# Second attention of a two-block transformer: blocks of 128 and of 256 keys share one step

## The reference, cut to what matters

```python
# NSA heads: a compressed branch, and two branches of softmax attention with a
# linear distance bias (here both see all of the 512 keys)
s = einsum('bgrqd,bgnd->bgrqn', q, k) * ATTN_SCALE - slopes * dist
p = softmax(where(dist >= 0, s, NEG_INF))
o = gate * einsum('bgrqn,bgnd->bgrqd', p, v)
...
# stick-breaking heads: the weight of key j is its sigmoid times the product of
# (1 - sigmoid) over the keys between j and the query
w[q, j] = sigmoid(s[q, j]) * prod(1 - sigmoid(s[q, l]) for l in (j, q))
o = einsum('qj,jd->qd', w, v)
```

## Time and profile before

| what | value |
|---|---|
| time, median of 3 runs | 1500.35 us (1496.9 to 1500.56) |
| the profiled execution: its time, its span | 1499.78 us, 1497.7 us |
| PE busy | 1453.9 us (97% of the span) |
| DVE busy | 948.2 us (63%) |
| ACT busy | 416.8 us (28%) |
| chain of work that ended last | PE 88%, DVE 7%, ACT 2%, issue 2% |
| second attention on PE (first scores to last output) | 760.30 to 984.60 us |

### The profile page before, as it was taken

How to read it: one execution, slowest core, us unless ns; L and a number is a source line. 1 busy time by engine, 2 the same in 40 slices (tenths; PEclk the granted TensorE clock), 3 DMA queues, 4 the chain that set the end, 5 groups by cost and what they waited for, 6 DMA issues and landing times.

```text
span 1497.7 us, 19514 instructions
## 1 busy us (share of the span) xinstructions
PE 1453.9 (97%) x7218; PEld 1171.0 (78%) x7218; DVE 948.2 (63%) x1705; ACT 416.8 (28%) x880; POOL 95.0 (6%) x75
## 2 busy tenths in 40 slices
PE   5999988999999999999999999999999999999997
PEld 5888866778888888888866666778887888888886
DVE  8787698876766665656556667874555445444443
ACT  5435444331111110003244456421113222221011
POOL 0000000110000000325200000000030000000110
PEclk9999999999999999999999999999999999999999
DMA  9353332445555655433211111123332223323332
GB/s 371 110 173 126 131 100 80 139 128 185 193 196 185 206 180 157 148 102 105 79 63 43 52 48 43 43 78 97 108 98 70 98 98 96 101 85 105 91 90 93
DMA packets 52609, 175.79 MB, mean 117 GB/s; under 512 B 5952, under 2 KB 6336, under 8 KB 52544
## 3 DMA queue, kind: packets, MB, share of 16 engines
q1 hardware_dynamic: 52544, 174.94, 35.7%
HBM read 172.82 MB, written 2.10 MB: 117 GB/s over the span
## 4 chain that ended last, share of the span: by engine, by line
PE 88%; DVE 7%; ACT 2%; issue 2%; DMA 0%; POOL 0%; SPq 0%; ACTq 0%; DVEq 0%
PE bank L650 20%; PE bank L652 19%; PE bank L651 19%; PE bank L1144 7%; PE bank L1163 2%; PE bank L1175 2%; PE bank L1198 2%; PE bank L826 2%; PE bank L824 2%; PE bank L825 2%; PE bank L997 1%; PE bank L858 1%; DVE wl L1694 1%; DVE ada L1714 1%; PE bank L662 1%
## 5 line engine op out<-in xcount | busy, mean ns | idle before, releaser
L650 PE MATMUL bank<-uh,wh 128*128 128x512 f32 x808 | 316.1, 391 | 6.0 <-DVE wl L1694 4.8
L651 PE MATMUL bank<-ul,wh 128*128 128x512 f32 x808 | 315.2, 390 | 0.0
L652 PE MATMUL bank<-uh,wl 128*128 128x512 f32 x808 | 315.2, 390 | 0.0
L1692 DVE CAST wh<-wraw 128x1024 fp32r<-128x1024 f32 (+1 forms) x223 | 147.9, 663 | 192.8 <-PE bank L652 179.9
L1694 DVE TENSOR_TENSOR wl<-wraw,wh 128x1024 fp32r<-128x1024 f32 (+1 forms) x223 | 260.3, 1167 | 7.7
L650 PEld LDWEIGHTS bank<-uh,wh 128*128 128x128 f32 x808 | 152.1, 188 | 39.0 <-issue 4.9
L652 PEld LDWEIGHTS bank<-uh,wl 128*128 128x128 f32 x808 | 152.1, 188 | 31.8
L651 PEld LDWEIGHTS bank<-ul,wh 128*128 128x128 f32 x808 | 152.0, 188 | 31.3
L650 PE MATMUL bank<-hh,wh 128*128 128x512 f32 x352 | 137.6, 391 | 0.0
L652 PE MATMUL bank<-hh,wl 128*128 128x512 f32 x352 | 137.1, 389 | 0.0
L651 PE MATMUL bank<-hl,wh 128*128 128x512 f32 x352 | 137.0, 389 | 0.0
(11 more groups left out here) (352 smaller groups left out, 2297.1 us busy)
## 6 DMA issues: line engine op xcount, KB each, us to landing
ada<-in_w_ada_dram SPq DMA_DIRECT2D x96, 512.0 KB, 4.6
wraw<-in_w_in_dram SPq DMA_DIRECT2D x61, 512.0 KB, 3.3
wraw<-in_w_ffn_gate_dram SPq DMA_DIRECT2D x44, 512.0 KB, 3.3
wraw<-in_w_ffn_up_dram SPq DMA_DIRECT2D x44, 512.0 KB, 3.3
wraw<-in_w_ffn_down_dram SPq DMA_DIRECT2D x32, 512.0 KB, 3.5
wraw<-in_w_ffn_down_dram SPq DMA_DIRECT2D x16, 384.0 KB, 3.1
wraw<-in_w_out_dram SPq DMA_DIRECT2D x16, 256.0 KB, 2.8
wraw<-in_w_out_dram SPq DMA_DIRECT2D x8, 512.0 KB, 3.4
```

What stands on the lines that cost most here:

```text
L650: nc.tensor.matmul(bank[:], a, rh[:, k0 + k, :], start=(first and k == 0), stop=False)
L651: nc.tensor.matmul(bank[:], a, rl[:, k0 + k, :], start=False, stop=False)
L652: mm = nc.tensor.matmul(bank[:], b, rh[:, k0 + k, :], start=False, stop=(last and k == nk - 1))
L1692: V.tensor_copy(wh[:, slot, 0:n], wraw[:, slot, 0:n]).then_inc(w_hi, 1)
```

## The change

The blocks of 128 and of 256 keys of one pair and branch now share a step: `PARTS = ((0, 1), (2,), (3,))`. Their scores stand side by side in one bank (columns 0 to 127 and 128 to 383, `place`), and so do their weights in `zt`, `kp`, `rb` and `wt2`. A pair and branch takes 3 steps of 384, 384 and 512 columns in place of 4 of 128, 256, 384 and 512; there are 24 NSA steps and 12 stick-breaking ones. The operations that need one row of bias, maximum, sum or running product for each query block (L2317, L1619, L2334, L2342, L2353, L2357) are still issued once for each block and head; the copies L1610 and the sigmoids L1630 and L1632 go over a step's columns in one instruction, and so do the small L2321, L2329 and L2331. Every step of attention now takes 12 fill matmuls, and two steps of 24 come behind the last one (`PORTIONS`). The number of matmuls, transposes and fill matmuls is the same as before.

```diff
-        NSA_TILES, ATT_TILES = 32, 48
+        NSA_TILES, ATT_TILES = 24, 36
+        PARTS = ((0, 1), (2,), (3,))
-        PORTIONS = [8, 8, 8, 12, 6, 6, 12, 12] * 4 + [8] * 3 + [12] * 12 + [8] * 3
+        PORTIONS = [12] * ATT_TILES + [24] * 2
...
+        def span_of(m):
+            return 512 if m % 3 == 2 else 384
+        def place(m, i):
+            first = P if i == 1 else 0
+            return slice(first, first + ZLEN[i])
...
             def pair_scores(m):
-                for ab in range(2):
...
-                    mm = nc.tensor.matmul(B[4 + 2 * (m % 2) + ab][:, 0:ZLEN[i]], q[:, i * P:(i + 1) * P], k[:, 0:ZLEN[i]],
-                                          start=True, stop=True)
+                for i in parts:
+                    for ab in range(2):
...
+                        mm = nc.tensor.matmul(B[4 + 2 * (m % 2) + ab][:, place(m, i)], q[:, i * P:(i + 1) * P],
+                                              k[:, 0:ZLEN[i]], start=True, stop=True)
                 mm.then_inc(a_z, 1)
...
             def pair_turn(m):
-                    for j in range(i + 1):
+                    for j in range(span_of(m) // P):
...
             def pair_output(m):
-                for j in range(i + 1):
+                for i, j in ((i, j) for i in parts for j in range(i + 1)):
+                    turned = slice(place(m, i).start + j * P, place(m, i).start + (j + 1) * P)
...
             def pair_taken(m):
-                    A(wt2[2 * (m % 2) + ab][:, 0:ZLEN[i]], B[2 + ab][:, 0:ZLEN[i]], ACT.Copy).then_inc(a_wt, 1)
+                    A(wt2[2 * (m % 2) + ab][:, 0:span_of(m)], B[2 + ab][:, 0:span_of(m)],
+                      ACT.Copy).then_inc(a_wt, 1)
             def pair_exps(m):
                 act.wait_ge(a_m, m + 1)
                 for ab in range(2):
-                    A(z, z, ACT.Exp, bias=nmx[:, c:c + 1], scale=SCALE,
-                      accum_out=sums[:, c:c + 1]).then_inc(a_e, 1)
+                    for i in work(m)[2]:
+                        c = 2 * i + ab
+                        z = zt[2 * (m % 3) + ab][:, place(m, i)]
+                        mm = A(z, z, ACT.Exp, bias=nmx[:, c:c + 1], scale=SCALE, accum_out=sums[:, c:c + 1])
+                    mm.then_inc(a_e, 1)
...
             def pair_sticks(m):
                 for ab in range(2):
                     v.wait_ge(sb_s, 4 * n + 2 * ab + 2)
...
-                    V.tensor_tensor_scan(r[:, ::-1], keep[:, ::-1], keep[:, ::-1], 1.0, ALU.mult,
-                                         ALU.bypass).then_inc(sb_r, 1)
+                    for i in work(m)[2]:
+                        keep = kp[2 * (m % 2) + ab][:, place(m, i)]
+                        r = rb[:, ab, place(m, i)]
+                        mm = V.tensor_tensor_scan(r[:, ::-1], keep[:, ::-1], keep[:, ::-1], 1.0, ALU.mult, ALU.bypass)
+                    mm.then_inc(sb_r, 1)
                     v.wait_ge(sb_r, 2 * n + ab + 1)
-                    V.tensor_tensor(sgm, sgm, r[:, 1:ZLEN[i]], ALU.mult).then_inc(a_w, 1)
+                    for i in work(m)[2]:
+                        pp = place(m, i)
+                        sgm = zt[2 * (m % 3) + ab][:, pp.start:pp.stop - 1]
+                        mm = V.tensor_tensor(sgm, sgm, rb[:, ab, pp.start + 1:pp.stop], ALU.mult)
+                    mm.then_inc(a_w, 1)
```

More of the change, by code:

```diff
@@ L332, in closes @@
                 return None
-            pair, br, i = work(m)
-            return pair if i == NT - 1 and br != 0 else None
+            pair, br, _ = work(m)
+            return pair if m % 3 == 2 and br != 0 else None
         MOD_AFTER = {PH["a1"].u0 + n + 1: [15 + n] for n in range(1, 9)}
@@ L1150, in pair_scores @@
             def pair_scores(m):
-                pair, br, i = work(m)
+                pair, br, parts = work(m)
                 if m >= NSA_TILES + 2:
@@ L1156, in pair_scores @@
                     pe.wait_ge(a_b, 2 * (m - 1))
-                for ab in range(2):
[L1158 to L1162, removed]
-                    mm = nc.tensor.matmul(B[4 + 2 * (m % 2) + ab][:, 0:ZLEN[i]], q[:, i * P:(i + 1) * P], k[:, 0:ZLEN[i]],
-                                          start=True, stop=True)
+                for i in parts:
+                    for ab in range(2):
+                        half = slice(64 * ab, 64 * ab + 64)
+                        if m < NSA_TILES:
+                            q, k = qa[half, pair, :], kdup[half, br, pair // 2, :]
+                        else:
+                            q, k = qkvb[half, pair - 4, :], qkvb[half, pair, :]
+                        mm = nc.tensor.matmul(B[4 + 2 * (m % 2) + ab][:, place(m, i)], q[:, i * P:(i + 1) * P],
+                                              k[:, 0:ZLEN[i]], start=True, stop=True)
                 mm.then_inc(a_z, 1)
             def pair_turn(m):
-                i = work(m)[2]
                 if m:
@@ L1179, in pair_output @@
             def pair_output(m):
-                pair, br, i = work(m)
-                first = i == 0 and br != 1
+                pair, br, parts = work(m)
+                first = m % 3 == 0 and br != 1
                 if first and pair:
@@ L1198, in pair_output @@
                         mm = nc.tensor.matmul(B[0][64 * ab:64 * ab + 64, i * P:(i + 1) * P], v,
-                                              wt2[2 * (m % 2) + ab][:, j * P:(j + 1) * P],
-                                              start=(first and br is None and j == 0),
+                                              wt2[2 * (m % 2) + ab][:, turned],
+                                              start=(i == 0 and br is None),
                                               stop=(closes(m) is not None and j == i), skip_group_check=True)
@@ L1206, in _ @@
             for m in range(ATT_TILES + 3):
-                if m == 4:
+                if m == 3:
                     pe.wait_ge(drain_a, PH["kv2"].a0 + 5)
@@ L2307, in pair_biased @@
             def pair_biased(m):
-                i = work(m)[2]
+                parts = work(m)[2]
                 v.wait_ge(a_z, m + 1)
@@ L2332, in pair_weights @@
                 for ab in range(2):
-                    z = zt[2 * (m % 3) + ab][:, 0:ZLEN[i]]
-                    V.tensor_scalar(z, z, rcs[:, 2 * i + ab:2 * i + ab + 1], None, ALU.mult).then_inc(a_w, 1)
+                    for i in parts:
+                        z = zt[2 * (m % 3) + ab][:, place(m, i)]
+                        mm = V.tensor_scalar(z, z, rcs[:, 2 * i + ab:2 * i + ab + 1], None, ALU.mult)
+                    mm.then_inc(a_w, 1)
             def pair_masked(m):
-                i = work(m)[2]
+                parts = work(m)[2]
@@ L2339, in pair_masked @@
                 v.wait_ge(a_z, m + 1)
                 for ab in range(2):
-                    zd = B[4 + 2 * (m % 2) + ab][:, i * P:(i + 1) * P]
-                    V.tensor_tensor(zd, zd, nst[:], ALU.add).then_inc(sb_m, 1)
+                    for i in parts:
+                        zd = B[4 + 2 * (m % 2) + ab][:, place(m, i).stop - P:place(m, i).stop]
+                        mm = V.tensor_tensor(zd, zd, nst[:], ALU.add)
+                    mm.then_inc(sb_m, 1)
             def pair_sticks(m):
-                i, n = work(m)[2], m - NSA_TILES
+                n = m - NSA_TILES
```

45 lines of the change are left out of this document (22 added, 23 removed).

## The result

The changed kernel takes 1490.9 us (median of 4 runs, 1490.56 to 1491.4) against 1498.97 (4 runs, 1496.9 to 1500.56). The ratio is 0.9946, 95% interval 0.9933 to 0.9958, so it is faster by 0.54%, some 8.1 us.

The account below looks back on a forecast made before the run. PE was taken to bound the attention; 4.0 us from twelve merged steps plus 1.9 from waits made 5.9 less than the profiled 1499.78, so 1493.9 us (0.4% faster), with a range of 1491.0 to 1498.5.

Parts of the forecast that it names:

- outputs, transposes and fill, twelve times: PE in twelve merged attention steps: outputs save 0.16, transposes -0.03, a fill group 0.20; 0.33 us each, 4.0 in all.
- scores' constant, in the eleven later ones: PE's scores in merged steps: each head's matmul carries its own 0.105 us, so merging saves nothing.
- second block's scores in the wait at the start: Start of attention: the 256-key block's scores (0.63 us) fall within PE's 2.2 us wait for key copies, saving 0.6.
- other waits: PE's short waits for value tiles (0.6) and, at the end, for last running products and copies (0.7) go.
- new waits: None booked: about 0.7 us left in NSA two-block steps, roughly half a microsecond at worst in the stick-breaking part.
- is the constant of the scores one for the group, or one for each matmul?: PE's two-block scores: 0.84 us if the group's, 1.05 if each matmul's; the prediction took 1.05.
- the rival made from it: Every constant on PE belongs to each instruction, so only the waits are saved: 1497.9 us, chance 0.16.
- three of the four kinds: PE's attention waits: the start's shortens by 0.6 us; value tiles (0.6), last products (0.5) and late copies (0.2) go.
- DVE becomes the bound: Stick-breaking part: DVE's 3.7 us idle per pair stays, a pair takes 18.6, ending at 1502.3 us; chance 0.10.
- The slower rival: NSA part: copies behind four exponentials make PE wait in each two-block step, ending at 1504.3 us; chance 0.06.
- the constants come back inside the merged steps: Within PE's merged groups each block change costs what a group change did; only waits go, 1497.9 us, chance 0.16.
- the group constant of the scores: PE's scores constant is the group's, so the steps' saving of 4.0 becomes 6.5 us, 1491.4; chance 0.10.

Follow-up runs that it names:

- e1: Changed kernel with a two-block step's scores issued as two groups, ahead of and behind the step's outputs; 1492.28 us, ratio to the kernel before 0.9949.
- e10: Kernel before the change, with only the scores of two steps issued together in every even step; 1493.78 us, ratio to the kernel before 0.9967.
- e2: Changed kernel with a two-block step's four score matmuls reordered, both blocks of one head first, then the other's; 1491.15 us, ratio to the kernel before 0.9941.
- e4: Changed kernel with fill given out earlier: 24 matmuls in steps 0 to 3, none behind the last scores; 1490.2 us, ratio to the kernel before 0.9948.
- e3: Changed kernel with every step's fill cut in two, 4 matmuls ahead of the transposes and 8 behind; 1492.47 us, ratio to the kernel before 0.9952.
- e8: Changed kernel with one unused 128x512 running product added on DVE ahead of each stick-breaking step's products; 1497.47 us, ratio to the kernel before 0.9989.
- e5: Changed kernel with a two-block step's outputs in two groups, ahead of and behind the scores; 1492.69 us, ratio to the kernel before 0.9959.

## Why the prediction was right in its direction and wrong in its size

| term | forecast us | measured us |
|---|---|---|
| outputs, transposes and fill, twelve times | 4.0 (0.33 each) | 12 x 0.51 = 6.1 with 12 x 0.2 of the scores, so 3.7 without them |
| scores' constant, in the eleven later ones | 0 | 2.2 (0.2 each; e1, e10) |
| second block's scores in the wait at the start | 0.6 | 0.6 |
| other waits | 1.3 | 2.0 (what is left of 8.5) |
| new waits | 0 | 0 |
| sum | 5.9 | 8.5 in the attention |

The step that failed is the question "is the constant of the scores one for the group, or one for each matmul?". I answered it with the two records that start half way to the next group, took them for the second head's matmul, and took that as proof of a half constant on each. Neither holds. By e2 the two heads run side by side, so the records that start together belong one to each head, and the start half way is the second record of both. And a group with two such starts can't tell the cases apart: a first one that pays for the entry and a last one that pays for the exit give the same picture as a half on each. The group with two blocks does. These are narrow cuts of the changed kernel's timeline at 827.05, 827.15 and 827.45, each showing what ran at that time:

```profile
826.87 0.50 PE L1174 MATMUL bank<-kdup,qa 64*128 64x128 f32 x4
...
826.98 0.39 PE L1174 MATMUL bank<-kdup,qa 64*128 64x256 f32 x2
...
827.20 0.38 PE L1174 MATMUL bank<-kdup,qa 64*128 64x256 f32 x2
```

Two records, one for each head, start at each of 826.65, 826.87, 826.98 and 827.20, and the outputs at 827.51. The intervals are 0.22, 0.11, 0.22 and 0.31: for 128 columns 0.22 when first and 0.11 when second, for 256 columns 0.22 in the midst and 0.31 when last. 0.1 us stand at each end of the group and nothing between. The scores are 2.2 of the 2.6 us that were missing; the waits add 0.7, and the other terms of the merged steps take 0.3 away.

The rule of the Trainium skill that was weighed ("TensorE: Matmul & The Clock Gate", "Back-to-back issue gap": weight load and matmul together set each matmul's spacing) was not the whole cost here. No run bears out the rival made from it: the number of matmuls never changed, and the attention's length went from 224.3 to 210.8 us. Within a group of scores the records agree with a fixed spacing (0.11 us for each 128 columns of a record, both heads at once); at a group's ends they show a second cost.

The wait terms: three of the four kinds went as forecast, and e4 shows that those at the end would come back without the fills of 24. What they were worth is 0.7 more than the idle times of the earlier trace rows, and most of that can be read from starts. The first pair is one of the waits of the kernel before, the second the same crossing from fill to transposes in e3, without a wait:

```profile
904.45 0.40 PE L1144 MATMUL bank<-uh,wh 128*128 128x512 f32 x1
905.12 1.09 PE L1175 MATMUL bank<-ident,zt 128*128 128x128 f32 x8 [0.27 <-ACT vbt L1571]
...
815.40 0.39 PE L1154 MATMUL bank<-uh,wh 128*128 128x512 f32 x1
815.63 1.03 PE L1185 MATMUL bank<-ident,zt 128*128 128x128 f32 x8
```

From start to start it is 0.67 us with the wait and 0.23 without, so the wait costs 0.44 where the list has 0.27. The list counts from the end of the record before, and records overlap when PE doesn't wait. Read in this way the four waits are worth 0.44, 0.44, 0.32 and 0.69, 1.9 us in all, where I had booked 1.3 from the list; about 0.1 stays open. e4 fits this: it loses 2.4 us where its list shows 2.1 of new idle time.

No new wait came, as forecast for both parts. The rival "DVE becomes the bound" failed at its price: it had the idle time of DVE stay, and e8 shows that it is used up when there is work. The slower rival didn't come up either: in no trace of the merged steps does PE wait for the copies in the NSA part. The rival "the constants come back inside the merged steps" is out by 0.81 for 12 output records in one group.

Last, the range. I had the group constant of the scores as a rival at 1491.4 with a chance of 0.10, and the range ended 0.4 below it. The 8.5 us of the attention, taken off the 1499.78 that the forecast started from, give 1491.3, inside the range by 0.3. That the median fell below the range, and by 0.1 only, is scatter of the other stages; what the forecast had wrong is the gain, 5.9 for 8.5.

## What to carry to other kernels

Where PE is busy all the time and its number of matmuls is fixed, look at how often it goes from one kind of work to another: here a merged step was worth 0.51 us, so 48 rounds of four groups had some 25 us of such costs (an estimate, 48 x 0.51). Read such a constant from groups of at least three different lengths and from a group with more than two starts, since with two "first and last" and "each" look the same. Find out which instruction a record belongs to before you reason from it, and measure what a wait costs from start to start, not from the listed idle time. Merge groups as long as the engines that live between them keep a margin, and measure that margin by adding work to them until PE waits.

## What the runs showed of the hardware that I had not expected

- Going between fill (128 rows, 128 columns of the array, 512 moving columns) and transposes (128 by 128 too) is nearly free: 0.05 us for a whole cut (e3). Going over to the scores (64 rows) and away from them costs 0.1 each, and a further group of outputs (64 columns) 0.15 (e1, e5). That the shape in the array is what counts fits all of these, but no run changed the shape alone.
- Score matmuls of two heads, which use different halves of the array's rows, run side by side: their records start in pairs, within 0.02 us, and in e2 the second head's 128 columns started ahead of the first head's 256, which the program issues before them.
- A stretch at the lower clock falls at different places in executions of unchanged code: within 690 to 700 us in five traces, within 738 to 748 in six, and in e1 within the attention (0.69 and 0.84 in two windows, 1.35 us lost there). What decides the place wasn't tried.
- The stages ahead of the attention vary by 5.5 us between executions of unchanged code, those behind it by 0.2. A change of 2 us can be read from a stage's length and not from a few whole times.
